# Two edits at the start of each mixture of experts: a later start for four weight loads, and 28 transposes ahead of the prompt's logits

## The reference, cut to what matters

```
h = h + mixer(rms_norm(h, mix_norm[i]))
h = h + expert_choice_moe(rms_norm(h, ffn_norm[i]), ...)
h = h + per_layer_embedding(h, ...)

aff = softmax(xt @ router_w)            # (tokens, 16)
gates, idx = top_k(aff.T, 2*tokens/16)  # each expert picks 32 prompt rows and 64 sample rows
xe = xt[idx]
ye = (silu(xe @ w_gate) * (xe @ w_up)) @ w_down * gates
y  = zeros.at[idx].add(ye)
```

## Time and profile before

| | us |
|---|---|
| median of 3 runs | 2458.11 (2456.77 to 2460.53) |
| the profiled execution | 2456.45 |
| its span | 2454.8 |
| PE busy | 2367.5 (96%) |
| mean granted clock of TensorE | 0.985 |

### The profile page before, as it was taken

The page is one execution under the profiler, slowest core; times in us unless marked ns, Lnnn a source line. Parts: engine busy times, 40 slices in busy tenths (PEclk is TensorE's granted clock), DMA queues, the critical chain, the costliest instruction groups (busy, mean ns, idle before and its releaser), DMA issues.

```text
span 2454.8 us, 33887 instructions
## 1 busy us (share of the span) xinstructions
PE 2367.5 (96%) x11934; PEld 1934.6 (79%) x11934; DVE 1742.6 (71%) x1989; ACT 1337.0 (54%) x1454; POOL 298.8 (12%) x360
## 2 busy tenths in 40 slices
PE   8999999999979999999999999998889999999997
PEld 6878788687768888888878888886678888888876
DVE  6545455344679888888866677766578888888854
ACT  4223222222447777777764455444157777777762
POOL 1000000000111221112111101000111111121011
PEclk9999999999989999999999999998889999999999
DMA  6424324132499999999972533332599999999931
GB/s 235 132 72 126 108 96 149 59 107 72 157 345 395 389 392 392 394 389 390 388 193 56 134 102 99 93 93 73 170 339 393 392 394 390 389 392 392 356 125 43
DMA packets 210961, 577.27 MB, mean 235 GB/s; under 512 B 24384, under 2 KB 65856, under 8 KB 210752
## 3 DMA queue, kind: packets, MB, share of 16 engines
q1 hardware_dynamic: 193584, 526.35, 57.5%
q0 software_dynamic: 17296, 49.83, 8.0%
HBM read 547.80 MB, written 30.43 MB: 236 GB/s over the span
## 4 chain that ended last, share of the span: by engine, by line
PE 91%; DVE 3%; DMA 3%; issue 1%; ACT 1%; POOL 0%; SPq 0%; DVEq 0%; POOLq 0%; ACTq 0%
PE bank L1557 43%; PE bank L1443 38%; PE bank L1372 4%; PE bank L1380 4%; PE bank L1743 1%; PE bank L1725 1%; DMA rows_normed<-xn_late 1%; DVE d_parts L613 1%; DMA m_x<-rows_normed,idx_t 1%; DMA resid<-in_x_sample 0%; DMA rows_summed<-m_y,idx_out 0%; DMA raw<-in_ret_w_in 0%; DVE top_i L1946 0%; DVE m_at L1948 0%; DMA resid<-rows_summed 0%
## 5 line engine op out<-in xcount | busy, mean ns | idle before, releaser
L2080 DVE TENSOR_TENSOR w_parts<-wt,w_parts 128x2048 fp32r<-128x2048 f32 x384 | 874.5, 2289 | 133.7 <-ACT w_parts L1133 125.3
L1133 ACT CAST w_parts<-wt 128x2048 fp32r<-128x2048 f32 x384 | 734.2, 1913 | 195.0 <-PE bank L1557 184.4
L1557 PE MATMUL bank<-w_parts,m_xt 128*128 128x512 f32 x2976 | 689.0, 390 | 2.1 <-ACT m_y L1191 2.1
L1557 PEld LDWEIGHTS bank<-w_parts,m_xt 128*128 128x128 f32 x2976 | 556.1, 188 | 117.2 <-issue 2.9
L1443 PE MATMUL bank<-d_parts,xt 128*128 128x512 f32 (+1 forms) x1872 | 388.0, 364 | 4.4 <-DVE d_parts L613 4.4
L1557 PE MATMUL bank<-w_parts,m_hidt 128*128 128x512 f32 x1632 | 382.7, 394 | 2.8 <-DVE m_hidt L2072 2.8
L1443 PEld LDWEIGHTS bank<-d_parts,xt 128*128 128x128 f32 x1872 | 316.0, 190 | 62.3 <-issue 7.4
L1557 PEld LDWEIGHTS bank<-w_parts,m_hidt 128*128 128x128 f32 x1632 | 306.1, 189 | 66.0 <-issue 3.3
L604 ACT CAST d_parts<-raw 128x512 fp32r<-128x512 f32 (+1 forms) x168 | 183.3, 1107 | 245.5 <-PE bank L1443 237.4
L613 DVE TENSOR_TENSOR d_parts<-raw,d_parts 128x512 fp32r<-128x512 f32 (+1 forms) x168 | 215.5, 1296 | 134.8 <-ACT d_parts L604 134.3
L1443 PE MATMUL bank<-xt,d_parts 128*128 128x256 f32 (+1 forms) x1536 | 284.1, 340 | 7.0 <-DVE xt L1803 2.9
(11 more groups left out here) (184 smaller groups left out, 2035.6 us busy)
## 6 DMA issues: line engine op xcount, KB each, us to landing
wt<-in_exp_w_gate SPq DMA_DIRECT2D x128, 1024.0 KB, 14.2
wt<-in_exp_w_up SPq DMA_DIRECT2D x128, 1024.0 KB, 13.1
wt<-in_exp_w_down SPq DMA_DIRECT2D x128, 1024.0 KB, 13.3
raw<-in_ret_w_in SPq DMA_DIRECT2D x32, 1024.0 KB, 5.2
raw<-in_na_w_in SPq DMA_DIRECT2D x24, 1024.0 KB, 5.4
raw<-in_ret_w_in SPq DMA_DIRECT2D x32, 512.0 KB, 4.5
raw<-in_ret_w_out SPq DMA_DIRECT2D x16, 1024.0 KB, 5.1
raw<-in_ple_w_gate SPq DMA_DIRECT2D x8, 1024.0 KB, 8.1
```

Of the source, the lines that this page charges most:

```text
L1133: nc.scalar.copy(w_parts[c % RING][:, 0, :], wt[:, place // 2, place % 2 * 2048:place % 2 * 2048 + 2048])\
L1557: last = nc.tensor.matmul(b[:, :], lhs[x][:, 2 * k + j, :], w[:, part, j, f * HALF:(f + 1) * HALF], start=(k == j == 0 and x == part == 0) ...
L2080: v.tensor_tensor(w_parts[c % RING][:, 1, :], wt[:, k // 2, k % 2 * 2048:k % 2 * 2048 + 2048], w_parts[c % RING][:, 0, :].bitcast(F32), AL ...
```

## The change

SP waits, in front of chunk c = 6 (the seventh) of the first expert of each layer, also for the landing of the two tiles of the prompt's normed rows. On PE, 28 transposes that nobody reads stand in front of the prompt's logits, in the bank (4) that the logits then write.

```diff
                     if c == 6:
                         sp.wait_ge(sample_out[l], 16 * 4)
+                        sp.wait_ge(rows_out[l], 16 * 2)
                     if c == 10:
                         sp.wait_ge(moe_rows[l], 16)
                     load(c, 0)
@@
             def mixture(l):
+                keep_busy(f"route{l}", ("lg", 0), 28)
                 logits(l, 0)
                 logit_tiles(l, 0)
                 affinities(l, 0)
```

## The result

| | median us | lowest to highest | runs |
|---|---|---|---|
| before | 2458.44 | 2456.77 to 2460.53 | 7 |
| changed | 2464.97 | 2460.26 to 2468.86 | 7 |

The ratio is 1.0028 (1.0018 to 1.0038): slower by 6.5 us, above my range. Of the 12.0 us between the two, 1.6 lie in the first 100 us, ahead of everything the change touches.

What follows compares the result with a forecast made beforehand. PE was taken as the bound, with 91% of the chain of waits. Layer 0's gather +2.0, layer 1's -2.2 and PE's start 0 made -0.2 us, a median of 2457.9, range 2454.4 to 2461.4.

Steps and rivals of the forecast that it cites:

- The 28 transposes, layer 0: Prompt's logits, layer 0: clock holds, 3.03 us instead of 4.52, so index and gather come 1.5 us sooner.
- The 28 transposes, layer 1: Prompt's logits, layer 1: worth 0, because the softmax waits for DVE's search of the sample; at most 2.7 us late.
- Layer 0's gather: First gather, layer 0: issued at 706.65 into a queue full of weights, landing at 716.3, +2.0 us.
- Layer 1's rows: Prompt's normed rows, layer 1: q0 alone moves the remaining 1.81 MB at 0.33 MB/us, landing about 1781.3, 10.4 us sooner.
- Layer 1's gather: First gather, layer 1: issued at 1790.1 into an almost empty queue, landing at 1796.65, -2.2 us.
- rival C: Both first gathers: held loads run into them, layer 1 +0.9, with layer 0 +2.9, median 2461.0; chance 20%.
- PE's start: First expert's slow first matmuls in each layer: change taken as 0, with +-1 us for each layer.
- The sum: Whole kernel: +2.0 - 2.2 + 0 = -0.2 us, a median of 2457.9.
- The rule on taking turns: Layer 0's gather: DMA engines alternate between queues, so its turn comes after 1.4 to 2.7 us, making +0.3 to +1.6.

Runs made afterwards that it cites:

- change_again: The changed kernel, unaltered, measured once more for its spread: ratio 1.0018 to the kernel before.
- change_tr0: The changed kernel with the 28 transposes in layer 0 alone: ratio 1.0023 to the kernel before.
- gains_later: The changed kernel with POOL's two loads of gains issued behind the first gather's landing instead of its issue: ratio 1.0032 to the kernel before.
- change_balanced: The changed kernel with the later group of unread transposes cut from 36 to 8 in layer 0: ratio 1.0012 to the kernel before.
- transposes_only: The kernel before plus the 28 transposes in both layers, without the added wait: ratio 1.0002 to the kernel before.

## Why the prediction was wrong

- **The 28 transposes, layer 0.** The sum of the logits was right (3.03 forecast, 2.97 measured, clock 1.00), and the gather left 1.8 us sooner behind n1. But I costed them at nothing but this gain and bounded them by "0 to -1.5". With 28 more of them in layer 0 a packet of instructions falls into a transfer on the path, and the stretch of the reload is 1.1 us longer on average; whether the slower matmuls behind it belong to that is open. No step of the sum had a place for it; I had named the work that hides their running time and nothing else they occupy.
- **The 28 transposes, layer 1.** Right: the index did not move, DVE's search ends it.
- **Layer 0's gather.** Right: +2.0 forecast, +2.3 to +2.6 measured in the changed kernels, by the mechanism forecast (full queue). Wrong was the aside that without the clock's gain it would be worse: by the text's own numbers that is 713.9 + 3.2, +2.8, and the wait alone gave +1.6.
- **Layer 1's rows.** This is the step that failed: "At 0.33: 5.5 us, landing about 1781.3". The second store landed 16.6 us after its issue, which is 1784.4 in before's time, 3.1 us later and beyond even my upper end of 1783.1. Two readings went wrong. I took c = 2 to 5 as through at 1775.4, since q1 had moved 4.19 MB by then. But a queue's total does not say whose bytes they are: in the kernel before, too, c = 5 was issued at 1763.6 and landed 16.7 us later, at 1780.3, so q0 had q1's last packets beside it for some 5 us more. And from the earlier trace rows I took the slices in the middle, "once started", and threw away the ramp and the tail, though the landing comes at the end of the tail; its average of 0.248 MB/us would have given 1783.1. 1.84 MB took 9.9 us. (My lower end, 1779.8, also left out the 0.4 us for the last receipts.)
- **Layer 1's gather.** Following from it, "almost empty", 6.5 us and -2.2, became full, 10.8 us and +2.0. That is rival C's mechanism with its threshold of 1784.4 just met; the landing was 15.8 to 18.2 us after the issue over the eight kernels with the wait in layer 1, 1783.6 to 1786.0, so to meet it so closely is luck. C's price of +0.9 was about right: in these eight kernels the rows came 0.4 us sooner to 2.0 later than before, 1.0 later on average, and the change's profile is the highest of them. Behind POOL's end the gather took 5.4 to 7.8 us where the price had 6.65. What spreads it is open. In the changed kernel q1's last packets of c = 6 to 9 and the rows' first transpose lie within 0.7 us of each other, in change_again they lie 1.9 apart.
- **PE's start.** 13.02 and 13.65 us in place of 12.49 and 12.94: +0.5 and +0.7, inside my +-1, but of one sign in both layers. In layer 0 it is more than chance of one profile: PE's first stretch takes 15.2 to 15.3 us in the two kernels whose layer 0 is that of before, and 15.6 to 16.8 in the sixteen others; a term put at 0 was +0.4 to +0.5 in the changed kernel and its repeats and +0.9 to +1.0 with the wait alone. Why is open.
- **The sum.** In the profiled execution, 12.0 us longer by its span, the landings are +2.3 and +2.0, the first experts' starts +1.2, the stretches at layer 0's embedding +0.9 (with the packet in the reload) and +2.5 (the slower matmuls behind it), together 8.9. The kernel's start gives 1.6, and the rest lies in stretches that differ as much between kernels whose code is the same there, such as 384.2 or 385.0 us through the attention. The +2.5 too is in part chance: from the embedding to the attention it was about 98.7, 100.2 or 101.2 us over all kernels. With 28 more transposes four kernels had 101.2 and four 100.2; without, five had 100.2 and five 98.7, the kernel before among the latter. The repeat of the change and its near twin, change_tr0, give 1.0018 and 1.0023, so +4.5 to +6.5 is the honest size. C had 20%. Its two terms made +2.9, and in the five kernels with both edits (change_tr0, gains_later and change_balanced among them) the rows come 3.5 us later on average. What C lacked up to the measured time stood in no rival's sum: PE's slower start, the reload, and stretches behind it that move by one or two microseconds from kernel to kernel.
- **The rule on taking turns** fits the row in kind: from issue to the gather's first packet it was 3.7 us with no weights left and 3.9 to 6.3 with them, so the turn came 0.2 to 2.6 us late, against the 1.4 to 2.7 us that I had estimated from the Trainium skill's page "DMA: Bandwidth & Descriptors", section "Queues, rings and completion order". The landing was later by more than that wait: in transposes_only the first packet came 0.2 us late and the landing 2.2. (By the same numbers layer 0 would have come out at +0.4 to +1.7, not +0.3 to +1.6; it was +2.3 and more.)

## What to carry to other kernels

Holding back a transfer does not take it off the queue, it moves it: work out what is in flight at the new time, and aim for the moment behind the short urgent transfer, with as few megabytes as the later work can spare (two chunks here, for some 0.1%, hardly clear of nothing, where four starved the second expert). Read the time of a landing from the landings of whole transfers, ramp and tail included, never from the rate in the middle or from the bytes that a queue has moved. Unread instructions lengthen the program as well as the time, so compare not only the stretch of the edit but every later stretch where a small transfer is on the path.

## What the runs showed of the hardware that I had not expected

- Instructions stand in the DMA trace as a queue of their own (q8), in 16 KB packets of 0.9 to 2.5 us; where one falls into the reload of the residual, the reload takes 3.5 to 4.0 us in place of 2.6 to 3.0. Its place in the work moved with 28 transposes more or fewer ahead of it.
- A first gather of 96 rows of 4 KB takes 6.0 to 6.6 us with no weights in q1 when POOL is done, and 7.7 to 10.8 where 1.7 to 3.2 MB of them are still to come at its issue. Issued 1.8 us sooner into such a queue, it landed no sooner.
- Small stores to rearranged rows end in a tail: the last 0.42 MB, alone, took 4.3 us, after 1.42 MB in 5.6 us beside the last of the weights.
- Four loads of 1 MB had moved their 4.19 MB, by the queue's total, 13.3 us after the first issue, but the last of them landed 18.2 us after it: later loads overtake it in the total.
